# Second norm split between ScalarE, GpSimd and VectorE; first tile gathered while the second one is chosen; first expert transfer moved ahead

## The reference

```python
x = x + gt1 * (merged @ w_out)
h2 = _rmsnorm(x, norm2_g) * (1.0 + sc2) + sh2
x = x + gt2 * _moe(h2, ...)          # 32 experts, the 4 largest logits of each token
return _rmsnorm(x, final_g)
# in _moe: logits = h2 @ router_w + router_b; weights = softmax over the 4 largest
#          expert: clipped gate and up (1024 -> 2 x 1024), product, down (1024 -> 1024)
```

## Time and profile before

| | |
|---|---|
| Median of 3 runs | 1346.03 us (1345.78 to 1346.28) |
| The profiled execution's own time | 1347.94 us |
| Its span, first to last instruction | 1346.2 us |
| GpSimd busy in the span | 703.6 us (52%) |
| VectorE busy | 478.4 us (36%) |
| ScalarE busy | 300.9 us (22%) |
| Bytes read from HBM | 482.40 MB |

### The profile page before, as it was taken

How to read it: one execution, slowest core, us unless ns; L and a number is a source line. 1 busy time by engine, 2 the same in 40 slices (tenths; PEclk the granted TensorE clock), 3 DMA queues, 4 the chain that set the end, 5 groups by cost and what they waited for, 6 DMA issues and landing times.

```text
span 1346.2 us, 18076 instructions
## 1 busy us (share of the span) xinstructions
PE 1320.4 (98%) x6683; PEld 620.1 (46%) x6684; DVE 478.4 (36%) x862; ACT 300.9 (22%) x577; POOL 703.6 (52%) x430
## 2 busy tenths in 40 slices
PE   7999999999999999999999999999999999999996
PEld 3888545788844333333333333333333333333332
DVE  1160006355578324223233242333332333233332
ACT  2320004310023222222122122222222222222222
POOL 1000000010015777767777687777777777777771
PEclk9999999999999999999999999999999999999998
DMA  9735333499959999999999999999999999999995
GB/s 339 279 127 186 125 125 125 161 322 367 329 219 382 429 428 429 428 403 429 428 428 428 428 409 429 428 428 428 407 431 428 428 428 407 430 428 428 428 427 231
DMA packets 70818, 483.79 MB, mean 359 GB/s; under 512 B 7270, under 2 KB 7466, under 8 KB 44970
## 3 DMA queue, kind: packets, MB, share of 16 engines
q1 hardware_dynamic: 69250, 478.20, 86.8%
q0 software_dynamic: 1056, 3.93, 1.0%
q10 hardware_dynamic: 488, 1.33, 0.3%
HBM read 482.40 MB, written 1.05 MB: 359 GB/s over the span
## 4 chain that ended last, share of the span: by engine, by line
DMA 56%; PE 34%; POOL 4%; issue 3%; DVE 1%; SPq 1%; ACT 1%; POOLq 0%; DVEq 0%; ACTq 0%
DMA landing<-in_w_gate_up 41%; PE bank L1332 15%; DMA landing<-in_w_down 14%; PE bank L1341 6%; POOL gu_slot L566 3%; PE bank L1688 3%; PE bank L1738 3%; PE bank L1574 2%; DMA piece<-in_w_ada 2%; SPq L397 1%; PE bank L1660 1%; PE bank L1553 0%; PE bank L1478 0%; PE bank L1705 0%; SPq L391 0%
## 5 line engine op out<-in xcount | busy, mean ns | idle before, releaser
L566 POOL COPY gu_slot<-landing 128x2048 f32<-128x2048 f32 x246 | 458.8, 1895 | 145.0 <-issue 107.9
L1688 PE MATMUL bank<-gu_slot,xg 128*64 128x512 f32 x2304 | 509.4, 593 | 3.2 <-POOL gu_slot L566 2.8
L1688 PEld LDWEIGHTS bank<-gu_slot,xg 128*64 128x64 f32 x2304 | 164.3, 137 | 320.5 <-issue 298.4
L566 POOL COPY dn_slot<-landing 128x2048 f32<-128x2048 f32 x120 | 223.5, 1894 | 71.2 <-issue 53.6
L1738 PE MATMUL bank<-dn_slot,actT 128*64 128x512 f32 x1152 | 255.1, 595 | 0.0
L1332 PE MATMUL bank<-hT,piece 128*128 128x256 f32 x704 | 153.4, 379 | 0.0
L1738 PEld LDWEIGHTS bank<-dn_slot,actT 128*64 128x64 f32 x1152 | 79.5, 137 | 159.2 <-issue 158.7
L1332 PEld LDWEIGHTS bank<-hT,piece 128*128 128x128 f32 x704 | 133.4, 190 | 19.1 <-issue 1.1
L812 ACT ACTIVATE ypart<-bank 128x512 bf16<-128x512 f32 x105 | 62.7, 597 | 313.8 <-DVE bank L1241 260.2
L1230 DVE TENSOR_SCALAR bank<-bank 128x512 f32<-128x512 f32 x36 | 25.2, 700 | 283.6 <-PE bank L1688 283.6
L1241 DVE SCALAR_TENSOR_TENSOR bank<-bank,slot_w,gt2q 128x512 f32<-128x512 f32 x35 | 26.6, 759 | 238.8 <-PE bank L1738 238.8
(11 more groups left out here) (342 smaller groups left out, 986.8 us busy)
## 6 DMA issues: line engine op xcount, KB each, us to landing
landing<-in_w_gate_up SPq DMA_DIRECT2D x123, 2048.0 KB, 10.7
landing<-in_w_down SPq DMA_DIRECT2D x60, 2048.0 KB, 10.7
piece<-in_w_in SPq DMA_DIRECT2D x17, 2048.0 KB, 7.7
piece<-in_w_ada SPq DMA_DIRECT2D x12, 2048.0 KB, 13.2
gu_slot<-in_w_gate_up SPq DMA_DIRECT2D x10, 1024.0 KB, 7.1
dn_slot<-in_w_down SPq DMA_DIRECT2D x8, 1024.0 KB, 13.8
piece<-in_w_branch_a SPq DMA_DIRECT2D x2, 2048.0 KB, 9.3
piece<-in_w_branch_b SPq DMA_DIRECT2D x2, 2048.0 KB, 8.1
```

What stands on the lines that cost most here:

```text
L566: nc.gpsimd.tensor_copy(place, landing[j // 2 % 3][:, j % 2, :]).then_inc(there, 16)
L1688: ins = M(gu_bank[u][64 * q:64 * q + 64, :], xg[:, k % 4, 64 * (k // 4):64 * (k // 4) + 64], gu_slot[k][:, cols_], start=(k == 0), stop=(k ...
```

## The change

- `second_norm` falls apart. For tile 0 VectorE still applies scale and shift (`first_rows`), out of a new buffer `u0`. For tile 1 ScalarE multiplies by the inverse root (two instructions of 128x512) and GpSimd adds `sh2` (two more), behind the router instead of ahead of it.
- The router works on the rows ahead of the norm: its logits are the inverse root times `u @ router_w`, plus a row `cb = sh2 @ router_w + router_b`. That row is a new tile `hc` (8 products with one output row, and the bias), spread over the partitions by one more product; `sh2` gets into column form by a store to HBM and a load of 1024 single elements on GpSimd's queue.
- Transposes come in the order `hh2`, `hh0`, `hh1`, `hh3`; then `rp0`, `rl0`, `rp1`, `rl1`.
- Ranks of the first expert have banks of their own; slots of tile 0 and its gather come while VectorE picks tile 1's four largest. Both `router_weights` and `chosen_of_slots` now stand ahead of the block counts, `first_used` right behind the counts, `subtract_part(1, 1)` ahead of the tables' last steps instead of behind them.
- The product `br` moves behind the first eighth of gate-up, `block_tables` from behind the first to behind the third.
- Of 25 idle `keep_busy` products 3 are left, ahead of the first gate-up.
- `gt2` is made in the two-halves form directly (`gt2q`); GpSimd's product with `bd` is 128x512 instead of 128x1024, and its two copies are gone. The sum `ab6` is gone from the sequence.
- `landing[0]` and `landing[1]` change places; unit 0 of expert 31 is issued right behind the first two pieces of expert 0. `dn_slot[3]` of expert 0 is loaded behind `rp1` instead of in the front part, since `h2T` now lies there.

```diff
             for q in (3, 0, 1, 2):
...
                 load_expert_piece(0, 2 * q + 1)
+                if q == 3:
+                    wait_tile(sp, "wb3")
+                    land(E - 1, 0)
-            sp.wait_ge(h2_ready, 4)
-            sp.wait_ge(gate_ready, 3)
-            land(E - 1, 0)
-            wait_tile(sp, "rl1")
+            wait_tile(sp, "rp1")
+            load_expert_piece(0, 11)
+            sp.wait_ge(h2_ready, 2)
+            sp.wait_ge(added_ready, 2)
+            sp.wait_ge(gate_ready, 1)
             land(E - 1, 1)
...
+            wait_out(pool, "ab3")
+            pool.dma_start(shift_store[:], sh2[0:1, :]).then_inc(shift_out, 16)
+            pool.wait_ge(shift_out, 16)
+            pool.dma_start(shc[:], shift_store[0].rearrange("(k p) -> p k", p=P), allow_slow_non_contiguous=True).then_inc(shc_in, 16)
...
+            wait_tile(pool, "wo3")
+            for i in range(2):
+                step(nc.gpsimd.memset(ypart[i][:], 0.0), ypart_ready[i])
+            for half in range(2):
+                cols_ = slice(512 * half, 512 * half + 512)
+                pool.wait_ge(scaled_ready, half + 1)
+                nc.gpsimd.tensor_tensor(h2[:, 1, cols_], h2[:, 1, cols_], sh2[:, cols_], ALU.add).then_inc(added_ready, 1)
             pool.wait_ge(wts_ready, TT)
...
+            act.wait_ge(rs1_ready, 1)
+            for half in range(2):
+                cols_ = slice(512 * half, 512 * half + 512)
+                A(h2[:, 1, cols_], h2[:, 1, cols_], ACT.Copy, scale=rs[:, 1:2]).then_inc(scaled_ready, 1)
...
+            logits(0)
+            four_largest(0)
+            logits(1)
+            choose_slots(0, rank0_full, bank[4][:, 0:1])
+            four_largest(1)
+            choose_slots(1, rank1_full, bank[3][:, 0:1])
             router_weights(0)
+            router_weights(1)
+            chosen_of_slots(first_slot[:, 0:1], first_slot[:, 1:2])
+            dve.wait_ge(added_ready, 2)
+            subtract_part(0, 1)
             wait_tile(dve, "rt")
...
+            step(V.tensor_scalar(first_used[:], blocks[0:1, 0:1], 1.0, None, ALU.add), first_count_ready)
...
-            router_weights(1)
+            subtract_part(1, 1)
             wait_tile(dve, "br")
...
-            keep_busy(a_bank, 3)
-            wait_out(pe, "br")
+            keep_busy(gu_bank[0], 3)
             pe.wait_ge(ident16_ready, 1)
-            gate_up(16, 1, (block_tables, weight_transposes))
+            gate_up(16, 1, {0: rank_blocks, 2: block_tables})
```

More of the change, by code:

```diff
@@ L1129, in _, with logits, four_largest @@
             step(V.memset(selT[:], 0.0), selw_out)
[L1130 to L1131 removed]
+            step(V.memset(ypart[2][:], 0.0), ypart_ready[2])
             step(V.memset(zrow[:], 0.0), zrow_ready)
+            subtract_part(1, 0)
             dve.wait_ge(numbers_ready, 1)
             step(V.tensor_scalar(esel[:], ones[0:3 * E, 0:SLOTS], expert_no[:], None, ALU.is_gt), esel_ready)
+            take_wo(3)
             step(V.memset(lg[:, :, E:E + TOP_K], PAD))
[L1137 removed]
+            norm_scale(1)
+            def logits(t):
                 wait_tile(dve, f"rl{t}")
[L1139 removed]
+                chain(V.scalar_tensor_tensor(lg[:, t, 0:E], tile(f"rl{t}")[:, 0:E], rs[:, t:t + 1], cb[:], ALU.mult, ALU.add), out_dve)
+            def four_largest(t):
                 chain(V.max(r8[:, t, :], lg[:, t, 0:E]))
@@ L1547, in _, with add_gate_parts @@
             attend(3)
+            def add_gate_parts():
+                ps = begin("ab7")
+                pe.wait_ge(modq_ready, 8)
+                for q in range(2):
+                    ins = M(ps[64 * q:64 * q + 64, :], ones[:, 0:64], modq[q][:], start=True, stop=True)
+                full(ins)
             def add_parts(r):
@@ L1565, in _ @@
                     by_feature(kind, cc, src)
-                    add_parts(r - 1)
+                    if r < 7:
+                        add_parts(r - 1)
                     r += 1
+            pe.wait_ge(late_in, 48)
+            pe.wait_ge(shc_in, 16)
+            ps = begin("hc")
+            for k in range(KT):
+                M(ps[0:1, 0:E], shc[:, k:k + 1], wr[:, k, :], start=(k == 0), stop=False)
+            full(M(ps[0:1, 0:E], ones[0:1, 0:1], rb[:], start=False, stop=True))
             pe.wait_ge(merged_ready, 4)
@@ L1576, in _ @@
                 if t == 0:
-                    add_parts(7)
+                    add_gate_parts()
+                    wait_out(pe, "hc")
+                    M(tile("hc")[:, 64:64 + E], ones[0:1, :], rb2[:], start=True, stop=True).then_inc(row_full, 1)
             pe.wait_ge(late_in, 48)
             pe.wait_ge(bias3_ready, 1)
-            for t in range(TT):
-                if t:
-                    keep_busy(tile("rp0"), 4)
-                for half in range(2):
-                    pe.wait_ge(h2_ready, 2 * t + half + 1)
-                    transposes(f"hh{2 * t + half}", h2, t, half)
+            pe.wait_ge(u_ready, 3)
+            transposes("hh2", h2, 1, 0)
+            pe.wait_ge(row_out, 1)
+            transposes("hh0", u0, None, 0)
+            transposes("hh1", u0, None, 1)
+            pe.wait_ge(u_ready, 4)
+            transposes("hh3", h2, 1, 1)
+            for t in range(TT):
                 ps = begin(f"rp{t}")
-                keep_busy(ps, 3 if t else 7)
                 for r in range(2):
@@ L1611, in _, with rank_blocks @@
             full(ins)
-            def gather(into):
-                for t in range(TT):
-                    for q in range(2):
-                        ins = M(into[64 * q:64 * q + 64, :], sel[:, t, :], h2[:, t, 512 * q:512 * q + 512],
-                                start=(t == 0), stop=(t == TT - 1))
-                ins.then_inc(gath_full, 1)
-            def gather_transposes(into):
-                for j in range(4):
-                    ins = nc.tensor.transpose(into[:, j * P:(j + 1) * P],
-                                              gx[:].rearrange("p (m i r) -> p m r i", m=2, r=2)[:, j // 2, j % 2, :], ident[:])
-                ins.then_inc(gxT_full, 1)
-            wait_out(pe, "rl0")
-            keep_busy(bank[6], 3)
-            pe.wait_ge(sel_ready, 1)
-            gather(x_bank)
-            pe.wait_ge(zrow_ready, 1)
-            for t in range(TT):
-                for q in range(2):
-                    M(sum_bank[t][q][:], zrow[0:1, 0:P], zrow[:], start=True, stop=False)
-            ps = begin("br")
-            pe.wait_ge(ranks_ready, 1)
-            full(M(ps[0:3 * E, 0:E], blocks_w[:], by_rank[:], start=True, stop=True))
             pe.wait_ge(gx_out, 1)
             gather_transposes(x_bank)
+            def rank_blocks():
+                ps = begin("br")
+                pe.wait_ge(ranks_ready, 1)
+                full(M(ps[0:3 * E, 4 * E:5 * E], blocks_w[:], by_rank[:], start=True, stop=True))
+                weight_transposes()
             def block_tables():
```

182 lines of the change are left out of this document (108 added, 74 removed), and 4 rows, old and new, of the table PLAN.

## The result

The changed kernel takes 1350.32 us (median of 7 executions, 1349.71 to 1350.56), the kernel before beside it 1346.27 us (7 executions, 1344.79 to 1350.28). The ratio is 1.0025, 95% interval 1.0015 to 1.0034, which is 2.0 to 4.6 us; the medians differ by 4.05 us. The prediction was 1346.9 us, no change beyond 0.2%; the time lies 1.4 us above the range and 1.1 us above the rival "the clock falls" (1349.2), whose sign in the trace is there. The profiled execution after took 1350.32 us, its span is 1348.6 us, 2.4 more than the earlier trace rows.

A forecast was written before the change was run, and what follows sets the result against it. DMA was taken as the bound, its stream full from unit 3 of expert 31. With unit 4 leaving at 428.45, unit 9 lands at 460.6 against 459.7: 1346.03 + 0.9 = 1346.9 us, range 1342.8 to 1348.9.

The forecast's parts named there:

- the clock falls: Rival: TensorE's clock at 0.50 between 412 and 420, +3.3 us, 1349.2 us; chance 0.12 together with an unseen wait.
- gate-up starts at 413.25, 2.1 earlier, first eighth done at 415.2: TensorE in the hand-over: gathers only tile 1 (0.97 us), then copy, transposes and copy (2.6), so gate-up starts earlier.
- Full from unit 4 to unit 9: Final sum over expert 31's stream: 428.5 + 2.7 + 6 x 4.9 = 460.6, against 459.7, so +0.9 us.
- The collision: Likeliest case, chance 0.45: VectorE's table steps wait for GpSimd's 1.9 us copies; unit 3 leaves at 422.15; 1346 to 1348.
- Test by unit 3 and those behind it: Test for every step: only what makes unit 3 of expert 31 and the units behind it leave earlier counts.
- Early unit 0 at 0: Queue: unit 0 in the hole, less `dn_slot[3]`, nets 2.45 us ahead of GpSimd's start; priced at 0.
- Unit 1 and 2: Queue: unit 1 waits for GpSimd's additions, unit 2 for `left`; they land by 416.2 and 421.1, before their copies; cost 0.
- Memsets at 0: Front part: GpSimd's two memsets at `wo3` beside VectorE's sums, between nothing and about 0.6 us, taken as 0.
- Second `sel` at 409.8: VectorE in the hand-over: tile 1's `sel` at 409.8, against 410.80 before; without collision 408.6.
- `ranks_ready` at 415.9 or, held, 417.8: VectorE's ranks: 415.9 undisturbed, 417.8 with `blocks_w` or `dump` held by GpSimd's copy 0 until 417.3.
- Fourth eighth at 424.8, unit 4 at 428.5: Gate-up: fourth eighth starts at 424.8, against 422.3 before, behind the tables; copy 3 ends and unit 4 leaves at 428.45.
- Pause of GpSimd between first and second copy: Expected sign in the profile: GpSimd's first copy near 415.4, then a pause before its second, which runs from 420.2.

The follow-up runs named there:

- e3: The kernel before without its 22 idle products between `wo3` and the gather; 1350.09 us, against 1347.32 us for the kernel before.
- e1: The changed kernel with 19 idle products put back into TensorE's waits of the hand-over; 1351.5 us, ratio 1.0035.
- e11: e1 with GpSimd's first copy made to wait for `by_rank` (the guard) and `subtract_part(1, 1)` behind `of_block`; 1350.05 us, ratio 1.0023.
- e7: The changed kernel with 14 idle products, `rank_blocks` behind the second eighth, `block_tables` behind the fourth, `subtract_part(1, 1)` behind the tables; 1352.24 us.
- e8: e7 with unit 0 of expert 31 issued behind `rp1`; 1351.44 us, ratio 1.0035.
- e4: e1 with GpSimd's two additions of `sh2` cut from 512 columns to 1 each; 1351.69 us, ratio 1.0032.
- e10: The changed kernel with denser idle products (23) and the later tables of e7; 1348.61 us, ratio 1.0022.
- e12: e11 with the denser idle products of e10; 1351.4 us, ratio 1.0048.
- e15: e11 unchanged, measured again beside e13 and e14; 1350.04 us, ratio 1.0024.
- e13: e11 with GpSimd's fifth copy made to wait until VectorE has written `pick`; 1350.22 us, ratio 1.0029.
- e14: e13 with `chosen_of_slots` moved from ahead of the block counts to behind the slot numbers; 1351.94 us, ratio 1.0036.
- e9: e1 with the later tables of e7; 1352.62 us, ratio 1.0048.

## Why the prediction was wrong

**The step that failed** is TensorE's in the hand-over: "gate-up starts at 413.25, 2.1 earlier, first eighth done at 415.2". It takes every duration from the earlier trace rows, that is at full clock, and leaves the clock to a rival with less than 12 in 100. Gate-up started at 416.93, 3.7 us later, and its first eighth ended at 419.42, 4.2 us later, although the front part was 1.1 earlier here than in the rows that the sum starts from. The rival had named the sign (0.50 between 412 and 420) and nearly the price: +3.3 foreseen, 3.0 found in the hand-over, 2.8 in e3. That the price fits is in part luck. The rival reached it by a fourth eighth 2.4 us late, which would hold back unit 4, and the fourth eighth was in time. My reason against it, that `rp` and `rl` "have 32 to 128 columns, and `zero_sums` follows", was wrong: the clock was 1.00 while they ran and fell at 407.9, behind eight microseconds in which TensorE had been busy for 4.99 (2.58 from 400 to 404, 2.41 from 404 to 408).

**The sum took the wrong unit.** It starts from unit 4 ("Full from unit 4 to unit 9"), and unit 4 left at 428.67, as foreseen (428.45). By the sum alone that is +1.1 us. But unit 3 left at 424.35 instead of 422.15, and the chain that ended last goes from unit 3 over its copy to unit 6 and to unit 9:

```profile
437.20 10.64 DMA landing<-in_w_gate_up
...
451.85 10.73 DMA landing<-in_w_gate_up
```

The prediction's own way of counting, begun at unit 3 (424.35 + 2.7 + 7 x 4.9), gives 461.4, which is 1.9 later than before; unit 9 landed at 462.58, 2.9 later. The prediction's test asked for unit 3 and those behind it, its sum then let unit 3 go. A slip beside it changes nothing: 410.9 + 2.6 is 413.5, not 413.25.

**The collision** was kept apart from the clock: I let the two exclude each other. With the clock low for 3.4 us only, unit 3 also leaves at 424.35 (e1), not at 422.15. Each can hold up unit 3 where the other is gone, and so e1 loses about as much as the change. Part of e1's delay is its own idle products (`rank1` waits behind four), so how much the collision alone costs in the changed kernel is not measured; the guard of e11, which takes it away, is worth 2.1 us at unit 3.

Point by point:

- *Test by unit 3 and those behind it*: right. Unit 3 is 1.9 later, the last pair 2.3, the span 2.4.
- *Early unit 0 at 0*: nothing speaks against it; e7 and e8 show it for a late start of GpSimd, within their scatter. *Unit 1 and 2*: issued in time.
- *Memsets at 0*: right; 0.98 us of them at 399.25 beside a sum of VectorE with two inputs that took 0.69, as the one at 401.11 in the earlier trace rows.

```profile
399.25 0.98 POOL L569 MEMSET ypart<- 128x512 bf16 x2 [11.21 <-PE bank L1646]
```
```profile
399.95 0.69 DVE L1084 TENSOR_TENSOR x<-xs,tmp 128x512 f32<-128x512 f32 x1
```

The Trainium skill, page "SBUF — State Buffer", section "Who interferes with whom", says that a VectorE operation with two SBUF inputs contends with a GpSimd instruction that reads SBUF, and not with one that only writes it; these rows agree, for the 0.28 us (399.95 to 400.23) in which they overlap.

- *Logits of tile 1 at 405.9*: 405.00. *`sel` of tile 0 held until 407.4*: held, 1.32 us in all, until 407.67. *`chosen` of tile 1 at 408.8*: written by 408.55. *Second `sel` at 409.8*: written by 410.79, no earlier than before (410.80); tile 1's rank waited in TensorE's order behind the first gather at half clock (407.81 to 409.74). Had the gather taken 0.97, `sel` would have been in time by my estimate.
- *Weights at 411.7*: GpSimd has them at 412.67. *`ranks_ready` at 415.9 or, held, 417.8*: 417.16, not held, since the first copy only came at 419.60 (foreseen 415.4). The hold that the prediction put there is in e1 and e4, 1.87 us, as sized.
- *Fourth eighth at 424.8, unit 4 at 428.5*: 424.64, and unit 4 leaves at 428.67. Right number, by another way: TensorE came late to the tables and did not have to wait for them.
- *Pause of GpSimd between first and second copy*: there, 0.93 us, but for a late TensorE.

**What stays open.** Why e10 to e12 and e15 end 1.8 to 2.2 us behind before's profile though unit 3 leaves at the same time. The rows place it: it is there when unit 12 leaves (464.78 before, 466.02 to 467.10 in these). The third place (VectorE held up to `pick`) is seen in the traces and lies on the chain of e11; that it carries these 2 us isn't shown, and neither e15 nor the times of e13 bear it out. No variant of the changed kernel came down to before's time. So it is shown that the fallen clock and the collision hold up unit 3, and not that they are the whole of the 4 us.

## What to carry to other kernels

Idle products are part of the schedule: whoever shortens the other engines' work around them takes every TensorE duration behind them at both levels of the clock, and asks which of the two the trace has a reason for. Starting an engine's long SBUF copies earlier is a gain only when the small steps of the other engine on the same memory are done; otherwise each of them can cost one copy, and the TensorE that waits for them may lose its clock besides (e4 and e14; not in e1 and e9). A sum over a chain of transfers starts from the unit that leaves last against its turn, so it is worked out from each of them. When an experiment removes one suspected loss and the time stays, look in its trace for the loss that took its place before dropping the suspicion.

## What was not expected of the hardware

- The same idle products have the clock back soon in one execution and late in another: e11 and e15 had 0.50 for 3.4 us, e13, the same up to there, for 17 us. Executions of one program differ by 5.6 us in e15 (1347.49 to 1353.07) and by 9.6 in e10 (1347.04 to 1356.68, the three slowest with the lowest mean clock), where the changed kernel's seven lie within 0.85 us.
- A stop of TensorE of 1.8 us (e4) or 2.39 us (e14) in the midst of 128x512 products is followed by 0.50 for 3.4 and 6.8 us, although the engine is fully busy by then. Stops of 1.81 us (e1) and 2.39 us (e9) in the same place are not. What tells them apart the traces do not show.
